# Sixteen short jobs among the projection tiles, three behind the last plain tile of each head chunk, and merged chunks kept in the space of their gates

## What is computed

```python
h = rmsnorm(x, g_norm)
z = h @ w_in                      # 8 fox heads, 8 diff heads: q, k, v, gate; forget logits; two merge gates
oa = rmsnorm(diff_attention(rope(qa), rope(ka), va, lam), g_subln) * (1 - lam_init) * silu(ga)
ob = forgetting_attention(qb, kb, vb, log_sigmoid(fl + b_f)) * silu(gb)
m = sigmoid(ma) * (oa @ w_proj_a) + sigmoid(mb) * (ob @ w_proj_b)
x = x + m @ w_out
return rmsnorm(x, g_final)
```

## Time and profile before

| | |
|---|---|
| median of 3 runs | 740.01 us (738.37 to 742.52) |
| profiled execution | 740.3 us, of which its span 738.5 us |
| TensorE matmul busy | 723.9 us, 98% of the span |
| TensorE weight load busy | 599.1 us, 81% |
| VectorE busy | 624.9 us, 85% |
| ScalarE busy | 462.8 us, 63% |
| GpSimd busy | 85.9 us, 12% |
| DMA | 178.39 MB, mean 242 GB/s |
| granted TensorE clock | 0.997 of full speed |

### The profile page before, as it was taken

The page is one execution under the profiler, slowest core; times in us unless marked ns, Lnnn a source line. Parts: engine busy times, 40 slices in busy tenths (PEclk is TensorE's granted clock), DMA queues, the critical chain, the costliest instruction groups (busy, mean ns, idle before and its releaser), DMA issues.

```text
span 738.5 us, 9450 instructions
## 1 busy us (share of the span) xinstructions
PE 723.9 (98%) x3454; PEld 599.1 (81%) x3454; DVE 624.9 (85%) x788; ACT 462.8 (63%) x682; POOL 85.9 (12%) x105
## 2 busy tenths in 40 slices
PE   9999999999999999999999999999999999999995
PEld 6998887868888888888888887888877888888884
DVE  6785698897989988989889899899899667799883
ACT  7963666567575766665865667776657544555552
POOL 0000231020202051000102030111030000001030
PEclk9999999999999999999999999999999999999998
DMA  8679356769676795776966867775768655667862
GB/s 334 211 235 322 125 199 229 245 242 349 217 259 229 239 348 208 261 234 235 326 228 216 270 226 260 281 257 202 225 233 266 214 192 191 279 232 246 285 200 114
DMA packets 49822, 178.39 MB, mean 242 GB/s; under 512 B 5544, under 2 KB 5552, under 8 KB 49264
## 3 DMA queue, kind: packets, MB, share of 16 engines
q1 hardware_dynamic: 48656, 174.41, 67.9%
q10 hardware_dynamic: 864, 1.84, 0.7%
q0 software_dynamic: 256, 1.54, 0.6%
HBM read 175.67 MB, written 2.11 MB: 241 GB/s over the span
## 4 chain that ended last, share of the span: by engine, by line
PE 46%; issue 28%; DVE 14%; DMA 6%; POOL 3%; ACT 2%; POOLq 0%; SPq 0%; DVEq 0%; ACTq 0%
PE Z L420 13%; PE Z L421 12%; PE Z L435 10%; DVE w_lo L956 7%; DMA w_raw<-in_w_main 4%; PE Z L488 3%; DVE x_and_g L971 3%; PE Z L594 3%; POOL rope_t L1385 1%; DMA gates<-c_rows_dram 1%; ACT w_hi L720 1%; DVE w_raw L969 1%; DMA c_rows_dram<-c_neg 1%; DVE sum_lo L1090 1%; POOL o_rstd L1397 1%
## 5 line engine op out<-in xcount | busy, mean ns | idle before, releaser
L956 DVE TENSOR_TENSOR w_lo<-w_raw,w_hi 128x1024 fp32r<-128x1024 f32 (+1 forms) x238 | 291.3, 1232 | 64.5 <-ACT w_hi L720 63.2
L720 ACT ACTIVATE w_hi<-w_raw 128x1024 fp32r<-128x1024 f32 (+1 forms) x237 | 245.4, 1044 | 134.9 <-PE Z L435 74.9
L420 PE MATMUL Z<-w_hi,hT_hi 128*128 128x512 f32 (+2 forms) x640 | 242.5, 382 | 2.6 <-ACT z_sb L725 2.3
L421 PE MATMUL Z<-w_hi,hT_lo 128*128 128x512 f32 (+2 forms) x640 | 240.3, 379 | 0.0
L720 ACT ACTIVATE w_hi<-x_and_g 128x1024 fp32r<-128x1024 f32 x88 | 93.2, 1062 | 95.5 <-DVE x_and_g L971 66.6
L420 PEld LDWEIGHTS Z<-w_hi,hT_hi 128*128 128x128 f32 x640 | 120.3, 188 | 26.8 <-ACT z_sb L725 3.1
L421 PEld LDWEIGHTS Z<-w_hi,hT_lo 128*128 128x128 f32 x640 | 120.4, 188 | 21.7
L435 PE MATMUL Z<-w_lo,hT_hi 128*128 128x512 f32 (+2 forms) x512 | 129.7, 376 | 0.0
L956 DVE TENSOR_TENSOR w_lo<-x_and_g,w_hi 128x1024 fp32r<-128x1024 f32 x88 | 108.4, 1233 | 13.0 <-ACT w_hi L720 11.5
L420 PE MATMUL Z<-w_hi,sum_hi 128*128 128x512 f32 x292 | 115.4, 395 | 1.4 <-DVE x_and_g L1193 1.3
L421 PE MATMUL Z<-w_hi,sum_lo 128*128 128x512 f32 x292 | 113.8, 390 | 0.0
(11 more groups left out here) (219 smaller groups left out, 698.5 us busy)
## 6 DMA issues: line engine op xcount, KB each, us to landing
w_raw<-in_w_main SPq DMA_DIRECT2D x295, 512.0 KB, 4.3
x_and_g<-in_w_main SPq DMA_DIRECT2D x22, 512.0 KB, 7.0
w_raw<-in_w_fl SPq DMA_DIRECT2D x8, 264.0 KB, 3.1
o_T<-in_x SPq DMA_DIRECT2D x1, 2048.0 KB, 8.0
x_and_g<-in_xT SPq DMA_DIRECT2D x4, 256.0 KB, 5.7
gates<-c_rows_dram POOLq DMA_DIRECT2D x1, 1024.0 KB, 8.4
z_sb<-in_g_final SPq DMA_DIRECT2D x1, 1024.0 KB, 10.0
x_and_g<-in_xT ACTq DMA_DIRECT2D x3, 256.0 KB, 7.3
```

Source lines behind the costliest of these rows:

```text
L420: pe.matmul(acc, a_hi, b_hi, start=first, stop=False)
L421: pe.matmul(acc, a_lo, b_hi, start=False, stop=False)
L720: act.activation(w_hi[:, t % RING, 0:cols_of(t)], weights(t), ACT.Copy).then_inc(hi_ready, 1)
L956: dve.tensor_tensor(w_lo[:, t % RING, 0:n], weights(t), w_hi[:, t % RING, 0:n].bitcast(fp32), ALU.subtract).then_inc(lo_ready, 1)
```

## The change

Of the 140 short jobs 124 stay in the head chunks: 12 in each of the first four, 11 in the next six, 10 in the last. In every chunk they alternate more evenly with the plain ones, and three follow the last plain job. The fox projection now has 32 jobs (240 to 271): four chunks of 4 plain jobs, each chunk followed by short ones, so that P3, P7, P4 and P2 of group 4 stand there; all four chunks use Z[0] and Z[1]. The number of jobs and their contents are the same. `fox_gate` writes its result over the gate it has used (`m_all` is now a view of `gates`). `form_taken` for P4 and P2 of group 4 moves ahead of the diff projection, which follows the last short job directly. Head 13 goes through `o_T` too (`SPLIT_HEADS` = 14), and the attention steps have new places.

```diff
--- before.py
+++ after.py
@@ -30,7 +30,7 @@
 PAIR_HEADS, PAIR_GROUP = (6, 7), 2
 P1, P5, P6, P3, P7, P4, P2 = range(FORMS)
 SUM_1, SUM_2, SUM_4, SUM_3 = range(4)
-SPLIT_HEADS = 13
+SPLIT_HEADS = 14
 FL_COL = 8 * WIDTH
 MERGE_COL = FL_COL + HEADS
 N_HEADS = 2 * HEADS
@@ -38,30 +38,33 @@
 
 FL_JOB, VG_JOB, PLAIN_JOB, MIXED_JOB = 8, 16, 20, 28
 ALONE = [h for h in range(N_HEADS) if h not in PAIR_HEADS]
-MIXED = 20
-FOX_JOB = MIXED_JOB + MIXED * (len(ALONE) - 3)
+SUMS_IN = [12] * 4 + [11] * 6 + [10]
+STEPS = {12: "hshsshshsshshshshsss", 11: "hshshsshshshshshsss", 10: "hshshshshshshshsss"}
+CHUNK_JOB = [MIXED_JOB]
+for n_sums in SUMS_IN:
+    CHUNK_JOB.append(CHUNK_JOB[-1] + TILES + n_sums)
+FOX_JOB = CHUNK_JOB[-1]
 FOX2_JOB = FOX_JOB + 16
-DIFF_JOB = FOX2_JOB + 8
+DIFF_JOB = FOX2_JOB + 16
 OUT_JOB = DIFF_JOB + 16
 LAST_JOB = OUT_JOB + 30
 JOBS = LAST_JOB + TILES
 
-HEAD_STEPS = (0, 3, 5, 8, 10, 13, 15, 17)
-SUM_STEPS = [u for u in range(MIXED) if u not in HEAD_STEPS]
-FOX_STEPS, FOX_SUM_STEPS = (0, 2, 4, 5, 8, 11, 14, 15), (1, 3, 6, 7, 9, 10, 12, 13)
+FOX_STEPS, FOX_SUM_STEPS = (0, 1, 3, 4, 8, 9, 11, 12), (2, 5, 6, 7, 10, 13, 14, 15)
 OUT_PLAIN = [(2, j) for j in range(TILES)] + [(0, j) for j in range(4, TILES)] + [(1, j) for j in range(4, TILES)]
 SUMS_BEHIND = [0, 0, 0, 2, 1, 1, 1, 1, 1, 1, 1, 1, 1, 1, 1, 1]
 OUT_ORDER = [kind for tile, sums in zip(OUT_PLAIN, SUMS_BEHIND) for kind in [tile] + ["s"] * sums]
 OUT_OF = {OUT_JOB + u: kind for u, kind in enumerate(OUT_ORDER) if kind != "s"}
 OUT_PLACE = {2: 0, 0: 1, 1: 2}
 OUT_DONE = {2: 0, 1: 1, 0: 2}
-SUM_JOB = ([MIXED_JOB + MIXED * c + u for c in range(len(ALONE) - 3) for u in SUM_STEPS] + [FOX_JOB + u for u in FOX_SUM_STEPS]
+SUM_JOB = ([CHUNK_JOB[c] + u for c, n_sums in enumerate(SUMS_IN) for u, kind in enumerate(STEPS[n_sums]) if kind == "s"]
+           + [first + u for first in (FOX_JOB, FOX2_JOB) for u in FOX_SUM_STEPS]
            + [OUT_JOB + u for u, kind in enumerate(OUT_ORDER) if kind == "s"])
 SUM_OF = {job: s for s, job in enumerate(SUM_JOB)}
-X_ALONE = {**{3 + c: MIXED_JOB + MIXED * (c + 1) + 4 for c in range(3)},
-           **{b: MIXED_JOB + 3 * MIXED + 4 + 16 * (b - 5) for b in range(6, N_HEADS)}}
-X_AT = {21: 0, 28: 1, 38: 2, **{job: b for b, job in X_ALONE.items()}, FOX2_JOB + 1: N_HEADS, DIFF_JOB + 1: N_HEADS + 1}
-Y_AT = {25: 0, 33: 1, 43: 2, **{job + 5: b for b, job in X_ALONE.items()}, FOX2_JOB + 5: N_HEADS}
+X_ALONE = {2: MIXED_JOB + 8, **{3 + c: CHUNK_JOB[c + 1] + 4 for c in range(3)},
+           **{b: CHUNK_JOB[3] + u for b, u in zip(range(6, N_HEADS), (19, 36, 49, 64, 80, 95, 112, 125, 140, 156))}, N_HEADS: FOX2_JOB + 1}
+X_AT = {21: 0, 28: 1, **{job: b for b, job in X_ALONE.items()}, DIFF_JOB + 1: N_HEADS + 1}
+Y_AT = {25: 0, 33: 1, **{job + 5: b for b, job in X_ALONE.items()}}
 
 C_ZERO, C_MASK, C_TRI, C_IDENT, C_ONE = 0, P, 2 * P, 3 * P, 4 * P
 C_COS, C_SIN, C_BF, C_GS, C_LAM = 5 * P, 5 * P + 16, 5 * P + 32, 5 * P + 40, 5 * P + 41
@@ -77,7 +80,7 @@
     c = ALONE.index(h)
     if c == 0:
         return j
-    return PLAIN_JOB + j if c == 2 else MIXED_JOB + MIXED * (c - 3) + HEAD_STEPS[j]
+    return PLAIN_JOB + j if c == 2 else CHUNK_JOB[c - 3] + [u for u, kind in enumerate(STEPS[SUMS_IN[c - 3]]) if kind == "h"][j]
 
 
 def max_count(heads):
@@ -85,7 +88,7 @@
 
 
 def fox_job(n, j):
-    return FOX_JOB + FOX_STEPS[4 * n + j] if n < 2 else FOX2_JOB + 4 * (n - 2) + j
+    return (FOX_JOB if n < 2 else FOX2_JOB) + FOX_STEPS[4 * (n % 2) + j]
 
 
 def diff_job(n, j):
@@ -93,7 +96,7 @@
 
 
 PARTS_AT = {PLAIN_JOB + 7: 0, MIXED_JOB + 2: 1, MIXED_JOB + 11: 2, MIXED_JOB + 18: 3}
-O_SPLIT_AT = {FOX_JOB - 20: 0, FOX_JOB - 11: 1, FOX2_JOB + 3: 2, FOX2_JOB + 4: 3}
+O_SPLIT_AT = {SUM_JOB[(GROUPS - 1) * FORMS * QUARTERS + 7] + 1: 0, FOX_JOB: 1, FOX2_JOB + 4: 2, FOX2_JOB + 5: 3}
 HEAD_OF = {head_job(c, j): (c, j) for c in ALONE[2:] for j in range(TILES)}
 FOX_OF = {fox_job(n, j): (n, j) for n in range(4) for j in range(4)}
 DIFF_OF = {diff_job(n, j): (n, j) for n in range(4) for j in range(4)}
@@ -227,7 +230,7 @@
         xT_sb = x_sb.rearrange("p (k n) -> p k n", k=KT)
         x_res = x_sb.rearrange("p (m n) -> p m n", m=M_TILES)
         chain = x_sb.rearrange("p (q n) -> p q n", q=QUARTERS)
-        m_all = x_sb.rearrange("p (n m c) -> p n m c", n=4, m=M_TILES)
+        m_all = gates[:, :, :, 1, :]
         x_res = o_T[:].rearrange("p h n -> p (h n)").rearrange("p (m n) -> p m n", m=M_TILES)
         x_sq = o_T[:]
         z_flat = z_sb[:].rearrange("p s m n -> p (s m n)")
@@ -638,13 +641,10 @@
 
             def fox_tile(n, j):
                 if j == 0:
-                    banks_free((16, 17, 17, 18)[n])
-                    if n == 2:
-                        form_taken(FORMS * GROUPS - 2)
-                        form_taken(FORMS * GROUPS - 1)
+                    banks_free(16 + n)
                 if n == 0:
                     pe.wait_ge(o_split, j // 2 + 1)
-                tile(fox_job(n, j), 1 if n == 2 else 0, oT_hi, oT_lo, 2 * j, 2, CHUNK, j == 0, j == 3)
+                tile(fox_job(n, j), 0, oT_hi, oT_lo, 2 * j, 2, CHUNK, j == 0, j == 3)
 
             for job in range(FOX_JOB, DIFF_JOB):
                 if job in FOX_OF:
@@ -655,11 +655,14 @@
 
             for n in range(4):
                 banks_free(19 + n)
+                if n == 0:
+                    form_taken(FORMS * GROUPS - 2)
+                    form_taken(FORMS * GROUPS - 1)
                 for j in range(4):
                     if n == 0:
                         pe.wait_ge(o_split, 3 if j < 2 else 4)
-                        if j >= 2:
-                            pe.wait_ge(oT_lo_ready, 1 if j == 2 else 3)
+                        if j == 3:
+                            pe.wait_ge(oT_lo_ready, 2)
                     tile(diff_job(n, j), 1 - n % 2, oT_hi, oT_lo, HEADS + 2 * j, 2, CHUNK, j == 0, j == 3)
                     attention(diff_job(n, j))
                     if j == 1 and n > 0:
@@ -1190,7 +1193,7 @@
                 dve.wait_ge(w_used, fox_job(n, 3) + 1)
                 dve.wait_ge(gates_ready, 4 * n + 2)
                 for m in range(M_TILES):
-                    dve.scalar_tensor_tensor(m_all[:, n, m, :], gates[:, n, m, 1, :], 1.0, Z[(2 if n == 2 else 0) + m][:],
+                    dve.scalar_tensor_tensor(m_all[:, n, m, :], gates[:, n, m, 1, :], 1.0, Z[m][:],
                                              ALU.add, ALU.mult).then_inc(evac[m], 1)
 
             def diff_gate(n):
```

## The result

The changed kernel took 741.44 us (median of 20 runs, 740.23 to 745.32) against 739.4 us of the kernel before (20 runs beside them, 736.97 to 743.02): ratio 1.0031, 95% interval 1.002 to 1.0043. That is 2.3 us slower by the ratio, where 3.9 us faster was forecast, and above the range. The profiled executions hide this: both took about 740.2 us (740.3 and 740.23), the one of before being slower than its median and the one of after the fastest of its runs. So each kernel was traced a second time.

What follows compares the result with a forecast made beforehand. TensorE's work plus its pauses was taken as the bound. From the profiled 740.3 us: -1.62 - 1.02 - 1.48 - 1.88 - 0.8 + 1.8 + 0.65 + 0.4 = -3.95, 736.35; as median 736.1 us, range 733.4 to 739.9.

Steps and rivals of the forecast that it cites:

- The four pauses that go: TensorE's pauses before h4.0, h14.0, f1.0 and at P7 of group 4 vanish: gains 1.62, 1.02, 1.48, 1.88 us.
- the rule of cover: At h4.0, h14.0, f1.0: three short jobs behind the last plain one give 4.1 us, hiding the late copy or gate.
- Evener mix in group 0: First chunks, jobs 57 to 62: 3 short and 3 plain jobs regain 0.8 of 1.7 us; bounds 0 and 1.7.
- The fold ahead of diff0.0: Before diff0.0, TensorE waits for VectorE's fold of P2, queued behind low parts: cost 1.8 us, bounds 0.7 and 3.5.
- The part of `o_T` at f0.2: At f0.2, TensorE waits for the second part of `o_T`, as VectorE comes late: cost 0.65 us, bounds 0 and 1.8.
- Small pauses: Longer projection stage, VectorE 89% busy: nothing charged but 0.4 us for small pauses.
- The yardstick: Between 285 and 450 us VectorE is 92% busy without visible TensorE pauses; taken as a share it can carry.
- P7 of group 4: P7 moves to 250-255 among plain jobs, Y15 just ahead of its adds: whole gain 1.88 us, bounds 0 and 1.88.
- Rival 3: Projection stage: late weights make VectorE the bound, with eight such waits at adds of P7 and P4: 744.6 us; chance 0.05.
- rival 2: P7's adds meet Y15 and chunk 1's gate; 1.9 us return, f0.2 waits 0.7 more: 738.7 us; chance 0.25.
- rival 1: New waits hidden: f0.2 costs 0, the fold 0.7, group 0 gives back all: 733.0 us; chance 0.18.
- Rival 4: At f0.2, GpSimd's rotation excludes VectorE by whole instructions, some 6 us: 742 us; chance 0.01.

Runs made afterwards that it cites:

- both edits: Changed kernel with P2 of group 4 covered by two plain jobs and the second part of `o_T` split ahead of job 244's weights: 736.94 us, ratio 0.997.

## Why the prediction was wrong

- *The four pauses that go* (-6.0): right as to their going, 6.0 and 5.0 us in two traces. The reason given for h4.0 was wrong in part: the earlier attention step does it too, and the third short job isn't needed. With both edits no copy pause came back with two short jobs behind every head, so the rule of cover was no guide.
- *Evener mix in group 0* (-0.8): wrong sign, and with 2.1 us the step that failed most. I counted VectorE's work over jobs 57 to 62 and overlooked that the three jobs behind the last plain one are all P4 there, 6.8 us of adds and low parts for 4.1 of TensorE. Measured +1.3 (2.6 against 1.6 and 1.0); giving this one chunk its old order brought 1.6 us in the runs.
- *The fold ahead of diff0.0* (+1.8, bounds 0.7 to 3.5): the mechanism was right, queue and all, and the size too small: 3.1 us in the runs, 2.22 and 3.48 in the traces. In the first trace the layout held as far as the fold: f3.3 ended at 592.50 and the fold at 598.33, 5.83 us later, where 5.75 was laid out. TensorE then began 0.46 us behind the fold, where I had 0.1. The second trace shows what else can come: I laid ScalarE's and VectorE's steps end to end and let every split start when TensorE freed its slot. The raw weights have a ring of four as well; a slot is loaded anew only after VectorE's low part, and a load takes 4.3 us to land (the median). There ScalarE waited 0.84 to 1.73 us for such loads, and the low parts and the fold behind them came later; whether late low parts or the loads themselves began it isn't shown. I had this only as a rival for the adds.
- *The part of `o_T` at f0.2* (+0.65): 1.4 us in the runs, 1.34 and 1.48 in the traces, behind a wait of 2.46 us for raw weights.
- *Small pauses* (+0.4): P4 of group 2 alone has 1.3 to 1.5, made by Y9 beside the adds. The yardstick was that VectorE can carry 92%; between 285 and 450 us it was now busy 147.88 of 165 us, 90%, and TensorE waited all the same. A mean over 165 us doesn't show a crowd of a few jobs.
- *P7 of group 4* beside Y15: right, no pause.

With the measured terms the sum is -5.5 + 1.3 + 3.1 + 1.4 + 1.4 = +1.7 us, against 2.3 measured; 0.6 us stay unexplained. Rival 3 named raw weights that land late, which is what stood ahead of the part of `o_T` and, in one trace, of the fold; it had the wrong place, since no add of P7 or P4 in the projection was what TensorE waited for. The range left the result out, and its ends don't fit its own reasons: rival 2 with the fold at its upper bound is 738.7 + 1.7 = 740.4, not 739.9, and rival 1's 733.0 lies below 733.4. The four terms that failed all erred to the same side: VectorE ran later than laid out. Rival 4 rested on a misreading of the earlier trace rows, of which more in the last section.

## What to carry to other kernels

When a wait is moved from behind long jobs to behind short ones, count what stands in the queue of the engine that must release it, and count each split there with the landing of its input, not only with its own duration; putting the one awaited instruction ahead of only the last of three low parts gave some 2 of 3 us in the runs without touching the order of the jobs. A short job that costs another engine more than it costs TensorE (2.28 against 1.365 us here) was cover where one or two stood together, and a debt where three that need an add did. And before adding cover, see what stands ahead of the late instruction in its own queue: at h4.0 moving an attention step was enough, and it made no new pause, where the third short job did.

## What the runs showed of the hardware

GpSimd and VectorE hold each other up, and most of it falls on GpSimd. In the changed kernel the bias of a head ran just ahead of P4 of group 0. GpSimd, then VectorE:

```profile
148.87 2.87 POOL L1371 TENSOR_TENSOR bias<-gates,c_nat 128x128 f32<-128x128 f32 x2 [28.53 <-DVE neg_max L1106]
151.82 2.73 POOL L1376 TENSOR_TENSOR bias<-bias,consts 128x128 f32<-128x128 f32 x2
```

```profile
149.84 1.43 DVE L959 TENSOR_TENSOR w_lo<-w_raw,w_hi 128x1024 fp32r<-128x1024 f32 x1
151.19 1.63 DVE L959 TENSOR_TENSOR w_lo<-x_and_g,w_hi 128x1024 fp32r<-128x1024 f32 x1
...
152.82 1.40 DVE L974 TENSOR_TENSOR x_and_g<-w_raw,x_and_g 128x1024 f32<-128x1024 f32 x1
154.14 1.48 DVE L959 TENSOR_TENSOR w_lo<-w_raw,w_hi 128x1024 fp32r<-128x1024 f32 x1
```

Four VectorE instructions took 5.94 us where four of 1.22 take 4.88, so 1.06 us went into the VectorE backlog just before those pauses; whether they depend on it wasn't tried, and in the kernel before two instructions beside the bias took 1.42 and 1.63, so 0.6 us of it was there already. GpSimd's instructions of 1.4 us are themselves held up. The same ones early in the changed kernel, with VectorE idle, and the rotation of an earlier head in the kernel before, nearly alone:

```profile
75.98 0.96 POOL L1371 TENSOR_TENSOR bias<-gates,c_nat 128x128 f32<-128x128 f32 x2 [7.97 <-DMA gates<-c_rows_dram]
77.02 0.89 POOL L1376 TENSOR_TENSOR bias<-bias,consts 128x128 f32<-128x128 f32 x2
```

```profile
285.41 1.17 POOL L1385 TENSOR_TENSOR rope_t<-z_sb,consts 128x64 f32<-128x64 f32 x4 [12.16 <-ACT z_sb L725]
```

So four bias instructions took 1.85 us alone and 5.60 beside VectorE, and four products of the rotation 1.17 alone and 4.20 beside it. VectorE lost 0.2 to 0.4 us for each of its instructions beside the bias (0.46 each alone) and 0.11 to 0.13 beside the rotation (0.3 each alone), each time less than one GpSimd instruction. The Trainium skill, "SBUF — State Buffer", section "Who interferes with whom", calls the ports that such a pair shares an exclusive lock. These rows fit it: neither engine loses more on an instruction than about one instruction of the other takes alone, and that is little for VectorE (0.3 to 0.5 us) and much for GpSimd (1.22). The prediction took 1.05 us for the length of a product of the rotation and found the rule contradicted by 0.11; that length was mostly waiting, and by 0.3 us for each of six instructions rival 4 would have been worth at most 1.8 us, not 6.
